# The first expert's up weights, asked for behind another item of the mixer

## What is computed

```python
def second_block(x, ...):
    h = rms_norm_2(x, norm_mix_w)
    p = h @ w_in
    y_rw  = rwkv7_mixer(p[..., :RW_COLS], ...)      # linear recurrence over 256 tokens, 8 heads of 64
    y_fox = fox_attention(...)                      # causal attention, 8 heads of 64
    x = x + concat([y_rw, y_fox]) @ w_out
    x = x + hierarchical_moe(rms_norm_2(x, norm_ffn_w), ...)

def expert_block(xblk, e):                          # one of 64 experts, chosen by two routers
    hid = silu(xblk @ w_gate[e]) * (xblk @ w_up[e]) # 1024 -> 512, twice
    return hid @ w_down[e]                          # 512 -> 1024
```

## Time and profile before

| | |
|---|---|
| timed runs, median (lowest to highest) | 1445.87 us (1445.66 to 1446.93) |
| span of the profiled execution, its own time on the profile | 1447.5 us |
| PE busy, DVE busy, ACT busy | 1086.3 (75%), 342.4 (24%), 217.3 us (15%) |
| bytes moved by DMA, mean rate | 463.40 MB, 320 GB/s |
| expert part starts (first request behind the barrier) | 525.34 us |
| first product of expert 0 | 536.00 us |

### The profile page before, as it was taken

The page is one execution under the profiler, slowest core; times in us unless marked ns, Lnnn a source line. Parts: engine busy times, 40 slices in busy tenths (PEclk is TensorE's granted clock), DMA queues, the critical chain, the costliest instruction groups (busy, mean ns, idle before and its releaser), DMA issues.

```text
span 1447.5 us, 35620 instructions
## 1 busy us (share of the span) xinstructions
PE 1086.3 (75%) x15906; PEld 777.4 (54%) x15906; DVE 342.4 (24%) x971; ACT 217.3 (15%) x598; POOL 69.0 (5%) x120
## 2 busy tenths in 40 slices
PE   7999999999999899765656655655665665666575
PEld 4876587646886767544444434444444444444443
DVE  2464256312663451111111011101111111111111
ACT  1163116301432021100000000000000000000000
POOL 1100010001021100000000000000000000000000
PEclk9999999999999799988888899888889888888988
DMA  8662245133220299999999999999999999999997
GB/s 286 231 207 71 90 151 199 30 133 117 84 93 4 76 399 427 428 430 430 431 430 430 431 430 431 429 430 431 430 431 429 430 431 430 431 431 430 431 429 316
DMA packets 69028, 463.40 MB, mean 320 GB/s; under 512 B 14789, under 2 KB 18278, under 8 KB 44390
## 3 DMA queue, kind: packets, MB, share of 16 engines
q1 hardware_dynamic: 64784, 459.77, 77.0%
q10 hardware_dynamic: 4182, 2.71, 0.7%
HBM read 461.41 MB, written 1.05 MB: 319 GB/s over the span
## 4 chain that ended last, share of the span: by engine, by line
DMA 54%; PE 9%; issue 1%; ACT 0%; DVE 0%; POOLq 0%; DVEq 0%; POOL 0%
DMA work_region<-in_exp_w_down_dram 54%; PE bank L2391 4%; PE bank L2382 2%; PE bank L2372 1%; PE bank L2408 1%; PE bank L2344 0%; PE bank L2360 0%; ACT work_region L2309 0%; DVE tokens L2577 0%; POOLq L2260 0%; ACT work_region L2305 0%; PE bank L2399 0%; DVE work_region L2555 0%; DVEq L2578 0%; PE bank L2349 0%
## 5 line engine op out<-in xcount | busy, mean ns | idle before, releaser
L2382 PE MATMUL bank<-weight_slots,work_region 128*32 128x128 f32 x5120 | 182.2, 302 | 125.5 <-DMA weight_slots<-in_exp_w_up_dram 100.8
L2382 PEld LDWEIGHTS bank<-weight_slots,work_region 128*32 128x32 f32 x5120 | 156.4, 121 | 153.1 <-DMA weight_slots<-in_exp_w_up_dram 111.1
L2391 PE MATMUL bank<-weight_slots,work_region 128*32 128x256 f32 x1376 | 115.3, 491 | 90.7 <-DMA weight_slots<-in_exp_w_down_dram 90.7
L2382 PE MATMUL bank<-work_region 128*32 128x128 f32 x2560 | 91.7, 304 | 60.8 <-DMA work_region<-in_exp_w_up_dram 52.1
L2391 PEld LDWEIGHTS bank<-weight_slots,work_region 128*32 128x32 f32 x1376 | 59.1, 135 | 132.9 <-issue 96.2
L2382 PEld LDWEIGHTS bank<-work_region 128*32 128x32 f32 x2560 | 78.6, 122 | 74.2 <-DMA work_region<-in_exp_w_up_dram 57.2
L2309 ACT COPY work_region<-bank 128x256 f32<-128x256 f32 x64 | 23.8, 373 | 603.8 <-PE bank L2391 603.8
L2544 DVE TENSOR_SCALAR work_region<-work_region 128x128 f32<-128x128 f32 x128 | 38.6, 345 | 281.1 <-PE bank L2399 281.1
L542 PE MATMUL bank<-weight_slots,normed_features 128*128 128x512 f32 (+2 forms) x288 | 102.6, 514 | 2.0 <-DVE normed_features L816 2.0
L2555 DVE TENSOR_TENSOR work_region<-work_region,bank 128x128 f32<-128x128 f32 x64 | 23.9, 374 | 285.6 <-PE bank L2382 285.6
L2391 PE MATMUL bank<-work_region 128*32 128x256 f32 x672 | 55.3, 483 | 43.0 <-DMA work_region<-in_exp_w_down_dram 43.0
(11 more groups left out here) (433 smaller groups left out, 1240.8 us busy)
## 6 DMA issues: line engine op xcount, KB each, us to landing
weight_slots<-in_exp_w_gate_dram SPq DMA_DIRECT2D x43, 2048.0 KB, 41.5
weight_slots<-in_exp_w_up_dram SPq DMA_DIRECT2D x43, 2048.0 KB, 41.0
weight_slots<-in_exp_w_down_dram SPq DMA_DIRECT2D x43, 2048.0 KB, 40.4
work_region<-in_exp_w_gate_dram SPq DMA_DIRECT2D x21, 2048.0 KB, 41.5
work_region<-in_exp_w_up_dram SPq DMA_DIRECT2D x21, 2048.0 KB, 40.7
work_region<-in_exp_w_down_dram SPq DMA_DIRECT2D x21, 2048.0 KB, 40.8
weight_slots<-in_w_in_dram SPq DMA_DIRECT2D x16, 2048.0 KB, 10.3
weight_slots<-in_w_out_dram SPq DMA_DIRECT2D x6, 2048.0 KB, 8.5
```

Of the source, the lines that this page charges most:

```text
L2382: mm = nc.tensor.matmul(B[bank][BLK * j:BLK * (j + 1), 0:P], x[:, c], w[u][:, c, j * P:(j + 1) * P], start=c == 0, stop=c == KC - 1, tile_ ...
L2391: mm = nc.tensor.matmul(B[7][BLK * j:BLK * (j + 1), 0:256], hidt[u][:, BLK * k:BLK * (k + 1)], w_down[u][:, k, j * 256:(j + 1) * 256], sta ...
```

## The change

SP asks for up 0 alone as soon as `item_made` reaches 17, the count of item TK1, and then goes on to the wait for the last outputs with what is left of `EARLY`, down 0 and gate 1. Nothing is added or taken away on any other engine.

```diff
             sp.wait_ge(S["rkv_done"], 6)
             load_first_experts(sp, a, mem, EARLY[0:1])
+            sp.wait_ge(S["item_made"], ORDER.index("TK1") + 1)
+            load_first_experts(sp, a, mem, EARLY[1:2])
             sp.wait_ge(S["bonus_ready"], MT)
             sp.wait_ge(S["y_made"], MT)
-            load_first_experts(sp, a, mem, EARLY[1:])
+            load_first_experts(sp, a, mem, EARLY[2:])
             for i in range(2):
                 sp.wait_ge(S["out_done"], 3 + i)
                 load_first_experts(sp, a, mem, LATE[i:i + 1])
```

## The result

The changed kernel takes 1448.2 us (median of 22 runs, 1445.18 to 1451.39) where the kernel before takes 1445.66 us in 22 runs beside it. The ratio is 1.0018 with a 95% interval of 1.0010 to 1.0025: 1.4 to 3.6 us slower, 2.6 us in the middle. That lies inside the forecast range; the forecast was 1446.2 us, and the forecast's own upper end, with no fall of the clock, was 1448.0 us. The step on which the prediction hung held, and one small term of its sum was six times too small.

A forecast was written before the change was run, and what follows sets the result against it. The prediction took the expert part as bound by a 430 GB/s DMA stream whose start PE and the barrier set. Terms 0 + 0 + 0 + 0.35 us on 1445.87 gave 1446.2 us, range 1443.9 to 1450.0 us.

The forecast's parts named there:

- The step on which the prediction hung: Mixer's end: DMA rate at or near zero from about 510 us until up 1's request near 515 us; gain 0.
- one small term of its sum: PE's instruction waits beside the early load in the mixer: put at +0.35 us.
- The stream: Loads behind 498.80 us end 4.9 us sooner, only lengthening the pause before up 1; gain 0.
- the 2 MB really leave the stream: Rival on the expert weight stream: the end comes 4.9 us sooner, 1441.0 us; chance 0.08.
- The request and SP's list: One transfer and one wait on SP, up 0 asked for about 55 us earlier, nobody held up; cost 0.
- Work under way beside the load: Near 443.5 to 449.5 us the load does not slow engines working beside it; cost 0.
- Instructions under the load: PE near 449 us: one or two instruction packets meet the load; +0.35 us, bounds -0.31 to +2.1.
- PE's wait near 449 us stays under 1 us: Sign for the changed profile: PE's issue wait in the mixer under the early load, 0.31 us before, stays small.
- The rule of the Trainium skill: Instruction blocks of 16 KiB are refilled mostly hidden; by it the sum would be 0 instead of +0.35 us.
- The slower rival: PE at 449 us: a wait grown to 2.42 us drops its clock; 1449.7 to 1456.8 us; chance 0.15.
- the forecast's own range: Whole kernel, no clock fall: 1443.9 us (wait at 470.61 vanishes) to 1448.0 us (longest wait under load).

The follow-up runs named there:

- e1: Against the kernel before: SP also waits for the turned key tiles, but up 0 is asked for where it was; ratio 1.0009.
- e4: Against the kernel before: up 0 asked for at the calm place, behind the first chunks' products, where PE's clock is at its lower level; ratio 1.0004.
- e6: Against the kernel before: up 0 asked for behind the last item of the list (WT1), in front of the chunks' fast products; ratio 1.0014.
- e8: Against the kernel before: gate 2, up 2, down 2 asked for in the pause before up 1, and up 0 behind the first chunks' products; ratio 0.9984.
- e9: Against the kernel before: gate 2, up 2, down 2 asked for in the pause before up 1, up 0 left where it was; ratio 0.9988.
- e0: The same change made once more, against the kernel before; ratio 1.0020.
- e2: Against the kernel before: up 0 asked for early, behind the turned key tiles, and once more at its old place; ratio 1.0027.
- e3: Against the kernel before: up 0 asked for early, as 8 transfers with 2 KB rows; ratio 1.0006.
- e7: Against the kernel before: another expert's matrix read early into up 0's slot for its traffic alone, then up 0; ratio 1.0021.
- e10: Against the kernel before: gate 2, up 2, down 2 asked for in the pause before up 1, and up 0 at the change's early place; ratio 1.0007.
- e5: Against the kernel before: only the first half of up 0 (1 MB) asked for early, the second half at the old place; ratio 1.0008.

## Why the prediction was right, and by how much it was off

**The stream.** Right: the 2 MB came off ahead of a pause. The prediction had the pause from about 510 us to up 1's request, 5 to 6 us long; it was 507 to 513 us in an execution that ran 2 us ahead. Expert to end did not move (911.5 and 911.6 us). The rival "the 2 MB really leave the stream" fell, and the filled pauses show how it could not have held even then.

**The request and SP's list.** Right: the wait alone leaves turn to turn at 13.47 us, and its time cannot be told from before.

**Work under way beside the load.** Right: in the calm place products keep their 309 ns. Wrong is how long the load lies there: 4.9 us at 430 GB/s in the prediction, but its packets begin between 440.3 and 447.2 us, and it takes 8.9 us from its request to landing. Gate 0, the load that the prediction cites as its like, had shown 8.3 us. The view of after from 439 to 449 us, and that of before from 415 to 426 us (KB, us to landing):

```profile
weight_slots<-in_exp_w_up_dram SPq DMA_DIRECT2D x1, 2048.0 KB, 8.9
```

```profile
weight_slots<-in_exp_w_gate_dram SPq DMA_DIRECT2D x1, 2048.0 KB, 8.3
```

**Instructions under the load.** This step named the right mechanism and the right place, and the failed part is the sentence that took "a value near the mean because the two stretches are like one another in this". The term was set at +0.35 us, one and a half packets at 0.23 us each, and measured +2.07 us from turn to turn, with one packet late; that is the upper end of its bounds (+2.1). The sign that PE's wait near 449 us stays under 1 us failed: it was 2.31 us. The mean over packets hid what decides: whether PE has work left when the packet is late. At the early place it has next to none: before, it waited 0.31 us for a packet that began 4.7 us behind the turning, and it waits for none that begins 4.0 to 4.4 us behind it (e1, e4, e6, e8 and e9). So 2.2 us of lateness become 2.0 us of wait; at the calm place a packet as late costs nothing that the profile shows. The reading of "issue" as a wait for instructions, offered as mine, now has the packet's own time behind it: in before and in after PE goes on 2.2 to 2.4 us behind the packet's start. The rule of the Trainium skill weighed there ("Runtime: NRT & Kernel Launch", section "Instruction fetch mechanics": the cost of a block is mostly hidden) agrees with the calm place and fails at the early one, by 2.0 us.

**The clock.** The slower rival needed a wait near 2 us and a fall of the clock behind it. The wait came, longer than the prediction wanted for it, and the fall did not: PE's clock stays at 1.00 from 440 us until the low stretch at 469.6 us. That the time stayed in the range is in this part luck: no reason of the prediction says why the clock should hold behind such a wait, and 1448.2 us lies 0.2 us above the end of the forecast's own range, inside the stated one only because that was widened for a fall of the clock that did not come. A wait of this length is not enough by itself: at this place it passed without a fall in all six kernels that have it at 2.0 us or more (after, e0, e2, e3, e7 and e10), while the second wait of the kernel with two loads, 2.20 us, has one behind it.

**What remains.** The sum with the right term is 1445.66 + 2.07 = 1447.7 us against 1448.2 us, well within the interval. The kernels without the long wait (e1, e4, e6, and e5 with its 0.86 us) stand at 1.0004 to 1.0014, none at or below 1; whether half a microsecond or one comes from something else in them is not settled by these runs.

## What to carry to other kernels

Taking a transfer out of a stream helps only if nothing upstream of the stream's next request pauses it: look for the first microsecond at which the queue is never empty again, and ask what releases the request there. When a large load is put beside dense small instructions, ask how much work the engine has left when its next instruction packet is due. A wait that it already has there with nothing shown marks a place with no slack, where a late packet is paid in full (0.31 us became 2.31); a place without one can have too little as well (the second wait of the kernel with two loads, 2.20 us). Where the engine worked at half the pace, a late packet cost nothing in one kernel and 0.38 us in another. A longer pause is an offer: here it took three other loads, and even that was worth only what the next bound, the first expert's own start, let through.

## What the runs showed that I had not expected

A weight load of 2 MB that keeps the DMA engines busy (a share of 0.95, 347 GB/s, from 440 to 446 us) delayed a 16 KB instruction packet by about 2 us, and in the one profile with smaller rows these did not help: with 2 KB rows the packet began 1.5 us sooner than in after but took 2.07 us instead of 0.93, for a wait of 2.02 us. Also, PE goes on about 2.2 to 2.5 us after the start of a packet of 0.93 us, whether it was late or not (before, after and the kernels e0, e2, e5, e7 and e10); counted from the packet's end it is 1.3 to 1.5 us in all of these, and 1.4 us in the kernel with small rows, whose packet was slow.
